# Experts' weights fetched two pieces at a time, 16 KB a partition, into five double places

## What is computed

```python
def expert_block(args):
    xb, e = args
    gate = xb @ w_gate[e] + b_gate[e]
    up = xb @ w_up[e] + b_up[e]
    gate = jnp.minimum(gate, SWIGLU_LIMIT)
    up = jnp.clip(up, -SWIGLU_LIMIT, SWIGLU_LIMIT)
    glu = gate * jax.nn.sigmoid(SWIGLU_ALPHA * gate)
    return (glu * (up + 1.0)) @ w_down[e] + b_down[e]
```

## Time and profile before

| what | value |
|---|---|
| median of 3 runs | 1760.61 us (1755.03 to 1762.65) |
| profiled execution, its own time | 1755.06 us |
| its span | 1753.7 us |
| TensorE granted clock, mean | 0.976 |

### The profile page before, as it was taken

How to read it: one execution, slowest core, us unless ns; L and a number is a source line. 1 busy time by engine, 2 the same in 40 slices (tenths; PEclk the granted TensorE clock), 3 DMA queues, 4 the chain that set the end, 5 groups by cost and what they waited for, 6 DMA issues and landing times.

```text
span 1753.7 us, 19425 instructions
## 1 busy us (share of the span) xinstructions
PE 1661.0 (95%) x7493; PEld 1258.4 (72%) x7493; DVE 1354.2 (77%) x1031; ACT 1206.6 (69%) x931; POOL 312.7 (18%) x162
## 2 busy tenths in 40 slices
PE   7999978999999999999999999999979999999998
PEld 5877856776676676676776776676744877778887
DVE  4576698999999999999999999999957324866343
ACT  4354457889889888889888888888852347564232
POOL 1402046421221221221221321321010000000000
PEclk9999979999999999999999999999987999999999
DMA  7311379999999999999999999999946221213221
GB/s 281 130 49 73 124 266 348 387 410 409 399 397 398 399 399 406 394 393 405 390 401 403 389 394 404 392 390 409 382 177 262 96 73 48 73 55 97 96 84 48
DMA packets 94574, 488.02 MB, mean 278 GB/s; under 512 B 12600, under 2 KB 14320, under 8 KB 44560
## 3 DMA queue, kind: packets, MB, share of 16 engines
q1 hardware_dynamic: 81696, 462.64, 67.6%
q0 software_dynamic: 8576, 18.34, 2.9%
q10 hardware_dynamic: 4208, 5.77, 1.0%
HBM read 478.00 MB, written 17.22 MB: 282 GB/s over the span
## 4 chain that ended last, share of the span: by engine, by line
PE 77%; DVE 10%; ACT 7%; issue 4%; DMA 1%; SPq 0%; DVEq 0%; POOLq 0%; ACTq 0%
PE PS L549 68%; ACT WH L1070 4%; PE PS L788 4%; DVE low L1418 3%; DVE WL L1418 3%; PE PS L1005 1%; DVE eu L1752 1%; DVE eu L1758 1%; PE PS L1017 1%; PE PS L802 1%; ACT ysl L1231 1%; DVE hl L1742 1%; DMA h2d<-HV 0%; PE PS L661 0%; PE PS L998 0%
## 5 line engine op out<-in xcount | busy, mean ns | idle before, releaser
L1070 ACT ACTIVATE WH<-land 128x2048 fp32r<-128x2048 f32 x210 | 396.0, 1910 | 131.1 <-PE PS L549 130.6
L1418 DVE TENSOR_TENSOR low<-ring,WH 128x2048 fp32r<-128x2048 f32 x194 | 437.1, 2285 | 37.0 <-ACT WH L1070 36.2
L1070 ACT ACTIVATE WH<-ring 128x2048 fp32r<-128x2048 f32 x218 | 410.8, 1911 | 72.9 <-PE PS L549 66.2
L1418 DVE TENSOR_TENSOR WL<-land,WH 128x2048 fp32r<-128x2048 f32 x190 | 427.9, 2285 | 33.8 <-ACT WH L1070 33.3
L549 PE MATMUL PS<-WH,xh 128*128 128x512 f32 x1024 | 310.5, 406 | 2.2 <-DVE xh L1740 1.5
L549 PEld LDWEIGHTS PS<-WH,xh 128*128 128x128 f32 x1024 | 191.2, 192 | 55.1 <-issue 6.5
L2084 POOL DMA_INDIRECT yd<-ys,lists x29 | 44.8, 1546 | 733.9 <-ACT ys L1255 733.9
L2061 POOL DMA_INDIRECT xg<-h2d,lists x29 | 157.1, 5418 | 8.8 <-issue 8.8
L549 PE MATMUL PS<-WL,xh 128*128 128x512 f32 (+1 forms) x532 | 155.0, 397 | 0.0
L549 PE MATMUL PS<-WH,hh 128*128 128x512 f32 x512 | 150.0, 394 | 1.5 <-DVE hh L1740 1.5
L549 PE MATMUL PS<-low,xh 128*128 128x512 f32 (+1 forms) x492 | 145.4, 402 | 0.0
(11 more groups left out here) (413 smaller groups left out, 2627.7 us busy)
## 6 DMA issues: line engine op xcount, KB each, us to landing
land<-in_w_up_dram SPq DMA_DIRECT2D x71, 1024.0 KB, 8.2
ring<-in_w_down_dram SPq DMA_DIRECT2D x71, 1024.0 KB, 8.4
ring<-in_w_gate_dram SPq DMA_DIRECT2D x66, 1024.0 KB, 7.6
land<-in_w_gate_dram SPq DMA_DIRECT2D x62, 1024.0 KB, 8.4
ring<-in_w_up_dram SPq DMA_DIRECT2D x57, 1024.0 KB, 8.2
land<-in_w_down_dram SPq DMA_DIRECT2D x57, 1024.0 KB, 8.9
ring<-in_w_in_dram SPq DMA_DIRECT2D x19, 1024.0 KB, 12.1
land<-in_w_in_dram SPq DMA_DIRECT2D x13, 1024.0 KB, 6.7
```

The source lines that it names most:

```text
L1070: A.activation(WH[buf[n]], lands[spot[n]], ACT.Copy).then_inc(s_hi, 1)
L1418: V.tensor_tensor(WLn[n], lands[spot[n]], WH[buf[n]].bitcast(F32), SUB).then_inc(s_lo, 1)
```

## The change

Two pieces next to each other in a matrix form a couple (g0 g1, g2 g3, g4 g5, d0 d1, g6 g7, d2 d3, in that order). A couple is 512 rows: partition p holds rows 4p to 4p+3, 16 KB in one run, and one DMA of 2 MB fetches it. The ten places are five double ones, each of 16 KB a partition; for that WH moves ahead of the ring in SBUF, and two WH and two WL buffers swap places. The DMA waits until both pieces in its double place have been used, and both of its pieces count as landed together. ScalarE, VectorE and TensorE still work by pieces. Since a partition holds four rows, each block of a turn takes every fourth feature, a step of 16 bytes. The places of the second block's first loads shift by one.

```diff
     CST = at[0]
     C = place("C", [128, NC1], F32)
     X = place("X", [128, 4, D], F32)
+    WH = [place(f"WH{i}", [128, 4, 512], F32R) for i in range(NS)]
     MEM_RING = at[0]
     ring = [place(f"ring{i}", [128, 4, 512], F32) for i in range(NR)]
-    WH = [place(f"WH{i}", [128, 4, 512], F32R) for i in range(NS)]
...
-    in_turn, later, later_low = [4, 0, 1, 2, 3, 5, 6, 7, 8, 9], (3, 5, 6), (7, 4, 0)
-    NL10 = len(in_turn)
-    spot = [n % NR if n < first else in_turn[(n - first) % NL10] if n < second else later[(n - second) % NS] for n in range(NP)]
+    later, later_low = (4, 5, 6), (7, 3, 0)
+    couples, couple_of = [], {}
+    for e in range(E + 1):
+        for what, p in items(e):
+            n = n_g[e, p] if what == "g" else n_d[e - 1, p]
+            if p % 2 == 0:
+                couple_of[n], couple_of[n_g[e, p + 1] if what == "g" else n_d[e - 1, p + 1]] = (len(couples), 0), (len(couples), 1)
+                couples.append((e, what, p))
+    NC5 = 5
+    spot = [n % NR if n < first else 2 * (couple_of[n][0] % NC5) + couple_of[n][1] if n < second else later[(n - second) % NS] for n in range(NP)]
...
+    wide = [place(f"wide{i}", [128, 4096], F32, MEM_RING + 16 * KB * i) for i in range(4)] + [reg("wide4", [128, 4096], F32, 69.5)]
...
+    def load_couple(c, ex):
+        e, what, p = couples[c]
+        two = [n_g[e, p], n_g[e, p + 1]] if what == "g" else [n_d[e - 1, p], n_d[e - 1, p + 1]]
+        for n in two:
+            wait_free(n)
+        if c == NC5 - 1:
             S.wait_ge(s_h2, 64)
...
+        w = w_down if what == "d" else (w_gate, w_up)[p // 4]
+        rows = 512 * (p % 4 // 2)
+        piece = w[0, 0, rows:rows + 512].rearrange("(p k) f -> p (k f)", k=4) if ex is None else \
+            w[0, bass.ds(ex, 1), rows:rows + 512].rearrange("a (p k) f -> p (a k f)", k=4)
+        S.dma_start(wide[c % NC5], piece).then_inc(s_couple[c % NC5], 16)
...
     def tensor_turn8(src, n):
-        pairs_ = src.rearrange("t (c p k) -> t c k p", p=128, k=2)
+        fours = src.rearrange("t (c p k) -> t c k p", p=128, k=4)
         for k in range(8):
             at_ = n * k
-            last = P.transpose(PS[:, 6 + at_ // 512, at_ % 512:at_ % 512 + n], pairs_[0:n, k // 2, k % 2], ident[0:n, 0:n])
+            last = P.transpose(PS[:, 6 + at_ // 512, at_ % 512:at_ % 512 + n], fours[0:n, k // 4, k % 4], ident[0:n, 0:n])
         last.then_inc(s_tt, 1)
...
-            A.wait_ge(s_land[spot[n]], landed(n))
+            A.wait_ge(s_land[n], landed(n))
             if before[n]:
                 A.wait_ge(s_mm, before[n])
-            A.activation(WH[buf[n]], lands[spot[n]], ACT.Copy).then_inc(s_hi, 1)
+            A.activation(WH[buf[n]], land_of[n], ACT.Copy).then_inc(s_hi, 1)
```

More of the change, by code:

```diff
@@ L241, in program @@
     pvk = reg("pvk", [128, 4, E, K], F32, 17)
-    WH += [reg(f"WH{3 + i}", [128, 4, 512], F32R, 53.5 + 16 * i) for i in range(2)]
-    WL += [reg(f"WL{3 + i}", [128, 4, 512], F32R, 61.5 + 16 * i) for i in range(2)]
+    WH += [reg(f"WH{3 + i}", [128, 4, 512], F32R, 53.5 + 8 * i) for i in range(2)]
+    WL += [reg(f"WL{3 + i}", [128, 4, 512], F32R, 69.5 + 8 * i) for i in range(2)]
     rk = reg("rk", [128, 3 * E], F32, 60)
@@ L317, in slot, with whole_rows @@
         return len(pieces) - w.shape[0] // 512
-    def whole_rows(w, kc):
-        pieces.append(w[256 * kc:256 * kc + 256].rearrange("(p k) f -> p (k f)", k=2))
+    def whole_rows():
+        pieces.append(None)
         done.append(done[-1] + 1)
@@ L342, in program @@
             if what == "g":
-                n_g[e, p] = whole_rows((w_gate, w_up)[p // 4][0, min(e, E - 1)], p % 4)
+                n_g[e, p] = whole_rows()
             else:
-                n_d[e - 1, p] = whole_rows(w_down[0, e - 1], p)
+                n_d[e - 1, p] = whole_rows()
     second = len(pieces)
@@ L365, in program @@
     lands = ring + [place(f"land{i}", [128, 4, 512], F32, LOWS + 8 * KB * i) for i in range(NS)]
-    lands += [reg(f"land{NS + i}", [128, 4, 512], F32, 61.5 + 16 * i) for i in range(2)]
+    lands += [reg(f"land{NS + i}", [128, 4, 512], F32, 69.5 + 8 * i) for i in range(2)]
     lows = [place(f"low{i}", [128, 4, 512], F32R, MEM_RING + 8 * KB * i) for i in range(NR)] + WL
-    in_turn, later, later_low = [4, 0, 1, 2, 3, 5, 6, 7, 8, 9], (3, 5, 6), (7, 4, 0)
-    NL10 = len(in_turn)
-    spot = [n % NR if n < first else in_turn[(n - first) % NL10] if n < second else later[(n - second) % NS] for n in range(NP)]
+    later, later_low = (4, 5, 6), (7, 3, 0)
[8 more added lines that the diff above has]
+    spot = [n % NR if n < first else 2 * (couple_of[n][0] % NC5) + couple_of[n][1] if n < second else later[(n - second) % NS] for n in range(NP)]
     low_spot = [NR + n % NS if n < first else spot[n] if n < second else later_low[(n - second) % NS] for n in range(NP)]
@@ L374, in program @@
     for n in range(NP):
-        count_[spot[n]] = count_.get(spot[n], 0) + 1
-        turns.append(count_[spot[n]])
+        where = (spot[n], first <= n < second)
+        count_[where] = count_.get(where, 0) + 1
+        turns.append(count_[where])
         prior.append(read.pop(spot[n], -1))
@@ L382, in program @@
         summed[low_spot[n]] = done[n + 1] if n not in (n_v, n_wm, n_v2) else done[n + 2] - 1
+    wide = [place(f"wide{i}", [128, 4096], F32, MEM_RING + 16 * KB * i) for i in range(4)] + [reg("wide4", [128, 4096], F32, 69.5)]
+    land_of = [wide[couple_of[n][0] % NC5][:, 2048 * couple_of[n][1]:2048 * couple_of[n][1] + 2048].rearrange("p (a f) -> p a f", a=4)
+               if first <= n < second else lands[spot[n]] for n in range(NP)]
     by_rows = lambda a: a.rearrange("p (k a) f -> p k (a f)", k=2)
@@ L469, in spread_out, with wait_free @@
         return V.tensor_reduce(o, e2, AX, ADD)
-    s_land = s_ring + [s_gpre, s_glog, s_gt, s_wz, s_wgh]
-    landed = lambda n: 16 * turns[n] + (1 if spot[n] >= NR else 0)
-    def load(n, piece=None):
+    s_couple = [s_gpre, s_glog, s_gt, s_wz, s_wgh]
+    in_couple = lambda n: first <= n < second
+    s_land = [s_couple[couple_of[n][0] % NC5] if in_couple(n) else s_ring[spot[n]] if n < first else s_ring[(n - second) % NS] for n in range(NP)]
+    start = [sum(1 for m in range(first) if spot[m] == i) for i in range(NS)]
+    landed = lambda n: 16 * turns[n] + 1 if in_couple(n) else 16 * (turns[n] if n < first else start[(n - second) % NS] + (n - second) // NS + 1)
+    def wait_free(n):
         if prior[n] >= 0:
@@ L480, in load @@
             S.wait_ge(s_mm, free[n])
-        if spot[n] >= NR + NS and turns[n] == 1:
-            S.wait_ge(s_h2, 64)
[L483 to L488, removed]
-    def sync_experts():
[L491 to L503, removed]
+    def load(n):
+        wait_free(n)
+        S.dma_start(lands[spot[n]], pieces[n]).then_inc(s_land[n], 16)
+    def load_couple(c, ex):
+        e, what, p = couples[c]
+        two = [n_g[e, p], n_g[e, p + 1]] if what == "g" else [n_d[e - 1, p], n_d[e - 1, p + 1]]
+        for n in two:
+            wait_free(n)
+        if c == NC5 - 1:
+            S.wait_ge(s_h2, 64)
+        w = w_down if what == "d" else (w_gate, w_up)[p // 4]
[3 more added lines that the diff above has]
+        S.dma_start(wide[c % NC5], piece).then_inc(s_couple[c % NC5], 16)
+    def sync_experts():
+        ex = last_ex = None
+        turn_ = 0
+        for c, (e, what, p) in enumerate(couples):
+            if e > turn_:
+                turn_, last_ex = e, ex
+                if e == 1:
+                    S.wait_ge(s_sig, 1)
+                if e < E:
+                    ex = S.value_load(sigi[0:1, e:e + 1], min_val=0, max_val=E - 1)
+            load_couple(c, ex if what == "g" else last_ex)
     def sync_first():
@@ L1417, in low @@
                 V.wait_ge(s_mm, low_free[n])
-            V.tensor_tensor(WLn[n], lands[spot[n]], WH[buf[n]].bitcast(F32), SUB).then_inc(s_lo, 1)
+            V.tensor_tensor(WLn[n], land_of[n], WH[buf[n]].bitcast(F32), SUB).then_inc(s_lo, 1)
     inverse = {}
```

## The result

The changed kernel takes 1789.99 us (median of 6 runs, 1785.45 to 1793.89) against 1760.95 us before (6 runs): a ratio of 1.0167, with a 95% interval from 1.0149 to 1.0185. That is 29 us slower. The forecast was slower, 1807 us. The profiled execution took 1793.89 us, the slowest of the six, and the one before 1755 us, the fastest of its six; the spans differ by 38.9 us, so the two traces show the loss a third too large.

What follows compares the result with a forecast made beforehand. The prediction took TensorE to pace the experts stage, with the turns on its path. To the profiled 1755.06 us it added 51 for the turns and 1 for the stage's start, giving 1807 us, range 1752 to 1829 us.

Steps and rivals of the forecast that it cites:

- What bounds the kernel: Experts stage: TensorE paces it, with the turns on its path; DMA engines at share 1.00 are full but not late.
- The turns: TensorE's transposes of line 788: weight loads at a 16-byte step lengthen each turn by 0.91 us, 56 turns counting, +51 us.
- first rival: TensorE's transposes: a 16-byte step costs what 8 bytes do, so nothing changes, 1755 to 1758 us; chance 0.15.
- The lost lead: Weight pieces in the experts stage: g6 lands 3.6 us late once an expert, covered by ScalarE's lead, so 0.
- third rival: g6's lateness passes through ScalarE to VectorE: 48 us, giving 1803 or 1855 us depending on the step's cost; chance 0.08.
- The fetch: Experts' weight DMAs: half as many at twice the size; nobody waits for the engines, so larger packets gain 0.
- second rival: DMA queue sets the pace and larger packets save 2.1%, 22 us over 16 pairs, giving 1733 us; chance 0.09.
- The start: Start of the experts stage: two couples go ahead of ScalarE's store in place of three pieces, 0 to 2.6 us, taken as +1.
- The sum: Whole kernel: 1755.06 + 51 + 1 = 1807 us, given unscaled.
- signs named: Observations that would confirm the forecast in the experts stage, among them a pair of experts near 69 us.
- the other sign: Transposes of line 788: turns of 1.8 to 2.1 us on the chain of waits would confirm the forecast.

Runs made afterwards that it cites:

- before_eight: The kernel before with eight places in place of ten, so every piece is asked for two pieces later: 1764.42 us, ratio 1.0019.
- halves_wait_both: The changed kernel with each couple as two 1 MB DMAs, each landing by itself, still waiting for both places: 1761.81 us, ratio 0.9994.
- couples_8k: The changed kernel with one 2 MB DMA and joint landing, but two packets of 8 KB and turns at the old 8-byte step: 1789.45 us, ratio 1.0169.
- all_halves: The changed kernel's layout, but every piece has its own DMA, asked for and landed alone in order of use: 1761.4 us, ratio 1.0004.

## Why the prediction was right in its direction and wrong in its reason

**What bounds the kernel** held. TensorE and what it waits for pace the stage. The DMA engines at a share of 1.00 were full but not late: couples took them to 0.97, and eight places left them at 1.00 with the time almost the same.

**The turns** are the step that failed. The prediction said that "a turn grows by 8 x (0.233 - 0.119) = 0.91 us" and made +51 us of it. The turns still take 0.95 and 1.10 us on the chain, where the clock is at its upper level, and the term was 0. The two rows that I leaned on were a sum on VectorE, whose price of 1.82 ns a number does not carry over to TensorE, and a difference between steps of 4 and 8 bytes, which turned out to be one jump and no slope: 140 ns at 4 bytes, then 209 at 8, 209 at 16, 194 at 32. My first rival, the free step, was the true half here. By the Trainium skill (SBUF — State Buffer, Door 1: The DMA port swizzle) a reader needs at least two hits in a line of 16 bytes, and 4 fp32 is how far it can step for free. The first of these spoke for a price of the change, the second against one. Neither is borne out for TensorE's weight loads by these numbers: the price comes at a step of 2 fp32, and 4 and 8 fp32 add nothing to it.

**The lost lead** was costed at 0, "ScalarE works up to four pieces ahead of TensorE, 11 us at 2.74, which covers this". This is the second step that failed; it measured 29 us. The third rival had named the piece, g6, and the reason. Two things were wrong in the cover. The mean of 2.74 us a piece hides that an odd expert's pieces take 8 matmuls instead of 12, and this is where it matters: the wait for `hh` occurs once a pair. And the four pieces are the lead of the rounding copies, but `hh` stands behind the copy of g6 and d1 in ScalarE's queue and had 0.8 us to spare, not 11. That rival priced what is left at 1.5 us an expert, 48 us, after taking off the time that VectorE had idled, which is no cover for `hh`. The loss is 29 us, some 1.9 us a pair (29 / 15.5). Which landing costs is shown by experiments; that it costs through `hh` is read from the traces, where time and place fit.

**How sharp the edge is** can be read from the runs. g6 asked for eight pieces ahead, alone: some 3 us, `hh` at most 3.6 us after the turn (before_eight). Asked for so late and behind d1: free, median 3.9 us (halves_wait_both). Behind g7 as well, 2.6 us more by the estimate in the prediction: the whole 29 us, median 6.0, with or without coupling. The edge lies at the 3.85 us above, and beyond it a delay counts in full.

**The fetch** was rightly costed at 0, for the reason given: the engines' time was not the limit. The second rival's saving of 2.1% did not come: 19016 us of engine time after, 18968 before. The Trainium skill (DMA: Bandwidth & Descriptors, Why small descriptors are slow) gives an operation 32 bytes of fixed data. The estimate from it that fits is 32 bytes in 16448, 0.2%, not the 0.4% of the prediction, which is the fixed share of one packet of 8 KB; no run here can show a difference of that size.

**The start** was +1 us. The first turn begins at 235.1 us instead of 232.9, 2.2 us later and within the 0 to 2.6 given. The other traces agree: 235.3 in couples_8k, 232.2 in all_halves.

**The sum** came out near by luck: a term of +51 that was nothing stood where one of +29 was missing. One of the signs named came near by the same luck: a pair of experts takes 68.1 us on average instead of 66.0 (350.38 to 1303.60 us after and 342.94 to 1266.44 before, 14 pairs each), against the 69 forecast. The turn of 1.98 us at 895.08 is not the other sign; it is the lower clock. The right number would have come from asking, for the piece with the shortest lead, what else is queued behind its copy.

A version with `hh` in front of g6's copy was not tried; it would settle the path through `hh`. Open is also why TensorE fell to its lower clock in 11 pairs instead of 8.

## What to carry to other kernels

When transfers are joined, look for the piece whose partner is not used right after it: it gets the partner's landing. Measure its lead in the fastest stretch, not by the mean, and follow the in-order queue of the engine that waits for it, because what stands behind may have far less lead than the piece itself. Measure that too, as here the time from the turn to `hh`. An idle engine's new waits mean nothing until one of them appears before the engine that sets the pace.

## What the runs showed of the hardware

- TensorE's loads of 128 fp32 columns took 140 ns for neighbouring elements, 209 and 216 at a step of 8 bytes, 209 and 215 at 16, 194 and 203 at 32 (medians), while VectorE's sum of 512 numbers at a step of 16 bytes took 1086 ns against 685 for neighbouring ones.
- With packets of 16 KB the SyncE queue took 19016 us of DMA engine time, with packets of 8 KB 18968 to 19094 (before, all_halves, couples_8k): no saving shows.
- After an idle time of 1.98 us TensorE's granted clock was 0.50 (1.2 GHz), and four matmuls took 2.04 us; at 1.00 (2.4 GHz), after the same idle time, they took 1.18.
